# A projection by pairs in the Winograd form: other places for loads, operand sums, staging buffers and attention's first transfers

## The reference

```
h = rmsnorm(x)
q, k, v, z_att, b, c, u, z_conv, g_att, g_conv = split(h @ W_in)
A = per head: softmax(rot(q) k') v, chunk-causal, two score maps, the second subtracted times lambda
att = rmsnorm(A) * silu(z_att);       yA = att @ W_att_out
cv  = b * conv3(c * u) * silu(z_conv); yB = cv @ W_conv_out
m = sigmoid(g_att + bias0) * yA + sigmoid(g_conv + bias1) * yB
x + rmsnorm(m @ W_out)
```

## Time and profile before

| | us |
|---|---|
| median of 3 runs | 1775.97 (1775.05 to 1779.68) |
| the profiled execution | 1778.97 |
| its span in the trace | 1777.1 |
| PE busy | 1717.4 |
| DVE busy | 1042.3 |
| ACT busy | 659.2 |
| POOL busy | 250.2 |

### The profile page before, as it was taken

How to read it: one execution, slowest core, us unless ns; L and a number is a source line. 1 busy time by engine, 2 the same in 40 slices (tenths; PEclk the granted TensorE clock), 3 DMA queues, 4 the chain that set the end, 5 groups by cost and what they waited for, 6 DMA issues and landing times.

```text
span 1777.1 us, 22838 instructions
## 1 busy us (share of the span) xinstructions
PE 1717.4 (97%) x8344; PEld 1434.3 (81%) x8344; DVE 1042.3 (59%) x2087; ACT 659.2 (37%) x1168; POOL 250.2 (14%) x178
## 2 busy tenths in 40 slices
PE   7999999998999986899999998999999999999998
PEld 6888888887788875688888887888888878888887
DVE  5538655648777775366766665676766453425242
ACT  5422333224332222144444454444445452323231
POOL 0000000069322312111101112110001040000000
PEclk9999999999999998899999999999999999999999
DMA  6547999653323244976567669657666875353532
GB/s 237 154 171 299 381 349 330 216 162 107 119 78 113 71 119 121 296 219 196 186 195 226 188 206 285 202 175 226 217 210 190 275 261 185 112 189 107 182 104 77
DMA packets 169435, 343.62 MB, mean 193 GB/s; under 512 B 16097, under 2 KB 61153, under 8 KB 163809
## 3 DMA queue, kind: packets, MB, share of 16 engines
q1 hardware_dynamic: 169314, 342.06, 60.5%
HBM read 230.84 MB, written 111.16 MB: 192 GB/s over the span
## 4 chain that ended last, share of the span: by engine, by line
PE 81%; DVE 6%; POOL 4%; DMA 4%; ACT 2%; issue 2%; SPq 1%; DVEq 0%; ACTq 0%; POOLq 0%
PE bank L1402 18%; PE bank L1225 12%; PE bank L1226 12%; PE bank L1227 12%; PE bank L1362 6%; PE bank L1334 3%; PE bank L1335 3%; PE bank L1345 3%; PE bank L1307 3%; PE bank L1310 3%; PE bank L1309 3%; DMA qk_s<-stage 1%; DMA gate_s<-gate_st 1%; DVE a_op L2000 1%; PE bank L1382 1%
## 5 line engine op out<-in xcount | busy, mean ns | idle before, releaser
L1402 PE MATMUL bank<-ht,w 128*128 128x512 f32 x912 | 239.1, 397 | 0.0
L2158 DVE CUSTOM_DVE_ANT_0 e<-bank,zeros 128x512 f32<-128x512 f32 x192 | 124.9, 688 | 131.8 <-PE bank L1335 131.3
L1402 PEld LDWEIGHTS bank<-ht,w 128*128 128x128 f32 x912 | 167.8, 190 | 32.3
L1307 PE MATMUL bank<-ht,a_op 128*128 128x512 f32 x392 | 156.5, 399 | 27.6 <-DVE bank L2031 9.8
L1700 ACT ACTIVATE e<-e,nbias 128x128 f32<-128x128 f32 (+15 forms) x128 | 153.7, 1200 | 76.7 <-DVE nbias L2167 76.6
L1225 PE MATMUL bank<-ht,w 128*128 128x512 f32 x448 | 174.4, 389 | 0.8 <-issue 0.8
L1227 PE MATMUL bank<-ht,w 128*128 128x512 f32 x448 | 174.3, 389 | 0.0
L1226 PE MATMUL bank<-ht,w 128*128 128x512 f32 x448 | 174.3, 389 | 0.0
L1209 POOL TENSOR_SCALAR mask<-kc,qc 128x128 f32<-128x128 f32 (+3 forms) x64 | 87.7, 1370 | 578.0 <-DVE mx L2158 577.5
L1309 PE MATMUL bank<-ht,a_op 128*128 128x512 f32 x392 | 155.1, 396 | 0.0
L1310 PE MATMUL bank<-ht,a_op 128*128 128x512 f32 x392 | 155.0, 395 | 0.0
(11 more groups left out here) (187 smaller groups left out, 3438.9 us busy)
## 6 DMA issues: line engine op xcount, KB each, us to landing
w<-split_s SPq DMA_DIRECT2D x124, 512.0 KB, 4.8
raw<-in_w_in SPq DMA_DIRECT2D x56, 512.0 KB, 5.7
split_s<-piece SPq DMA_DIRECT2D x24, 1024.0 KB, 5.7
q_st<-qk_s SPq DMA_DIRECT2D x128, 128.0 KB, 4.7
gate_s<-gate_st SPq DMA_DIRECT2D x64, 256.0 KB, 5.2
ring<-gate_s SPq DMA_DIRECT2D x64, 256.0 KB, 3.4
ht_s<-ht SPq DMA_DIRECT2D x6, 2048.0 KB, 9.6
qk_s<-stage SPq DMA_DIRECT2D x48, 192.0 KB, 3.5
```

Of the source, the lines that this page charges most:

```text
L1307: nc.tensor.matmul(out[:], hi, right[:, k, 0, :], start=k == 0 and not adds, stop=False, skip_group_check=adds)
L1402: mm = nc.tensor.matmul(bank[2 + u % 2][:], unit_weights(u)[:, term // 2, k, :], h_slot(bb, k)[:, term % 2, :], start=i == 0, stop=i == PE ...
L2158: nc.vector.tensor_tensor_reduce(e[:, c:c + wide], bank[(0, 1, 4)[o % 3]][:, 0:wide], mask[m % 2][:, 0:wide] if masked else zeros[:, 0:wid ...
```

## The change

Eight edits, none of which adds or removes an operation on data:

1. `S_SUMS`: POOL forms S1, S2, S3, S4 in this order (it was S1, S3, S2, S4). For pairs 0 and 1 S1 and S2 stand in front of T4, S3 and S4 behind it.
2. POOL forms T3 first, from the end of tile 19's block 1 on (it waited for tile 22's block 1); T1 keeps that wait and comes second.
3. T2 lies in `u2[0]`, `u2[1]`, `tmp[2]`, `s_3[1]`; so `take_p1(1)` waits for nothing of T4 any more, and U2 of the first pairs for 14 counts of `t_sum`.
4. DVE forms U2 in front of the first two splits of a single pair.
5. SP loads pair q + 3 between the stores of blocks 2 and the stores of blocks 3 of pair q (it loaded pair q + 2 ahead of all of them); pair 4 ahead of the stores of (0, 3) and (2, 3).
6. The staging buffer of a block is two further on.
7. Before attention SP loads only the first chunk of k, stores (25, 3) and (27, 3), loads units 0 and 1, stores (25, 2) and (27, 2), and then loads the other three chunks of k.
8. v's first chunk is loaded behind the stores of (24, 2) and (26, 2).

```diff
-S_SUMS = ("S1", "S3", "S2", "S4")
+S_SUMS = ("S1", "S2", "S3", "S4")
...
-    return AT[p - 1 if kind_of(p) == "conv" and place_of(p) == 3 else p, b] % 4
+    return (AT[p - 1 if kind_of(p) == "conv" and place_of(p) == 3 else p, b] + 2) % 4
...
-        t_2 = [p1[1]] + u2 + [tmp[2]]
+        t_2 = u2 + [tmp[2], s_3[1]]
...
-        T_SUMS, T_ORDER = (1, 3, 2, 4), (1, 2, 3, 4)
+        T_SUMS, T_ORDER = (3, 1, 2, 4), (1, 2, 3, 4)
...
-            for b, x in ((3, 1), (2, 1), (3, 0)):
+            for b, x in ((3, 1), (2, 1)):
                 for q in (0, 1):
                     store_block(2 * q + x, b)
+            for x in range(2):
+                load_half_pair(4, x)
+            for q in (0, 1):
+                store_block(2 * q, 3)
             for q in range(2, X):
-                for x in range(2):
-                    load_half_pair(q + 2, x)
...
-                for b in (2, 3):
+                for x in range(2):
+                    store_block(2 * q + x, 2)
+                if q + 3 < LINE_PAIRS:
                     for x in range(2):
-                        store_block(2 * q + x, b)
+                        load_half_pair(q + 3, x)
+                for x in range(2):
+                    store_block(2 * q + x, 3)
...
-            for c in range(0, S, BLK):
-                load_k(Plan(True), 0, c)
-            sp.wait_ge(proj_done, product_at(POS[Y, "P7"]))
+            load_k(Plan(True), 0, 0)
+            for q in (X, Y):
+                store_block(2 * q + 1, 3)
             load_unit(0)
             load_unit(1)
             for q in (X, Y):
-                store_block(2 * q + 1, 3)
-            sp.wait_ge(proj_done, product_at(POS[Y, "P4"]))
-            load_v(Plan(True), 0, 0)
-            for q in (X, Y):
                 store_block(2 * q + 1, 2)
+            for c in range(BLK, S, BLK):
+                load_k(Plan(True), 0, c)
...
             for q in (X, Y):
                 store_block(2 * q, 2)
+            load_v(Plan(True), 0, 0)
...
-            pool.wait_ge(dve_done, done_at(QK_P + 2, 1))
+            pool.wait_ge(dve_done, done_at(QK_P - 1, 1))
...
-            for x in (1, 3):
-                for k in range(4):
-                    t_sums(x, k)
-            pool.wait_ge(t_sum, 4)
+            for k in range(4):
+                t_sums(3, k)
+            pool.wait_ge(dve_done, done_at(QK_P + 2, 1))
+            for k in range(4):
+                t_sums(1, k)
+            pool.wait_ge(t_sum, 8)
...
-            for x in ("S1", "S3"):
+            for x in ("S1", "S2"):
                 for q in (0, 1):
                     s_sums(q, x)
             for k in range(4):
                 t_sums(4, k)
-            for x in ("S2", "S4"):
+
+            pool.wait_ge(t_sum, 16)
+            for x in ("S3", "S4"):
                 for q in (0, 1):
                     s_sums(q, x)
...
                 if q >= 2:
                     act.wait_ge(sum_done, SUM_POS[q - 2, "U2"] + 1)
-                elif q == 1:
-
-                    act.wait_ge(t_sum, 13)
-                    act.wait_ge(ht_lo_done, 2 * NT + 5)
...
-                    dve.wait_ge(t_sum, 15)
+                    dve.wait_ge(t_sum, 14)
...
                 i = POS[q, ONE_PAIR[0]] + A_SLOTS
-                split_a(i)
-                split_a(i + 1)
                 form_u2(q)
-                split_a(i + 2)
+                for j in range(3):
+                    split_a(i + j)
                 form_u3(q)
                 form_c22(q)
                 split_a(i + 3)
```

## The result

The changed kernel takes 1769.05 us (median of 8 runs, 1765.3 to 1771.46) against 1777.0 (8 runs, 1775.05 to 1783.6): ratio 0.9943, 95% interval 0.9927 to 0.996. It is faster: by 8 us between the medians, by 0.57% (10 us) by the ratio. A gain of 23 us was forecast, and the time lies above the range. The profiled execution took 1770.07 us, its span is 1768.2.

The account below looks back on a forecast made before the run. TensorE was busy in 97% of the span, so time could come only from its idle and half-speed stretches. 3.2 + 2 + 9.1 + 9 - 0.3 = 23 us took the median from 1775.97 to 1753, range 1747 to 1764.

Parts of the forecast that it names:

- (a): Line's start: T3 first, T2 elsewhere, S2 in front of T4 bring P6 of pair 0 to 443.3, gaining 3.2 us.
- (c): Line's end: loads one pair sooner bring P5 of pair 13 to 679.4, gaining 9.1 us (7 to 10.5).
- S2 in front of S3: POOL's sums: 1.6 us less DVE waiting for P6's factor, within (c); nothing in single pairs, within (b).
- (b): Single pairs: U2 in front of the two splits removes TensorE's waits for U2, gaining 2 us (1 to 3).
- (d): Attention's start: stores in front of its loads, staging buffers turned by two, gaining 9 us (3 to 11).
- The end stays bound by transfers: Attention's start: late first weights or (26, 2) at 742 and later; (d) gives 2, total gain 16, 1760 us; 15%.
- The slow rival: Pairs' loads in front of stores of blocks 3 delay these, ACT waits for staging; 36 us lost, 1789 us; 3%.
- Those named for the line: Signs: P6 of pair 0 at 442 to 445; P3 of pair 11 waits 2 to 4 us, P5 of pair 13 8 to 10.
- the wrong side: Signs against, at attention's start: a DMA row in TensorE's waits (first weights), a 4 us wait for the maxima still there.

Follow-up runs that it names:

- load_old: Changed kernel with the old loop of loads and stores (pair q + 2 loaded ahead of pair q's stores): 1774.88 us, ratio 0.9984 to the kernel before.
- t1_first: Changed kernel with T1 formed first again and T3 behind it, both from tile 22 on: 1773.74 us in its one run.
- s3_before_s2: Changed kernel with S3 in front of S2 again for pairs 2 to 13: 1766.72 us in its one run.
- u2_old: Changed kernel with U2 behind two splits again: 1765.96 us in its one run.
- k_in_gap: Changed kernel with k's other three chunks loaded right behind the first, in the sync queue's waiting time: 1760.54 us, ratio 0.989 to the kernel before.
- line_only: Changed kernel with attention's old queue and the old staging buffers, keeping only the line's edits: 1764.82 us, ratio 0.992 to the kernel before.
- turn_old_queue: Changed kernel with attention's old queue, keeping the line's edits and the turned staging buffers: 1759.77 us, ratio 0.9883 to the kernel before.
- no_turn: Changed kernel without the turn of the staging buffers: 1774.47 us, ratio 0.9975 to the kernel before.
- last_order: turn_old_queue with the last two pairs reordered: P5, P1, P6 of pair 12, then of pair 13, then by turns: 1756.45 us, ratio 0.988 to the kernel before.

## Why the prediction was wrong

**Steps (a) and (c) held, to the microsecond.** P6 at 442.79 against 443.3 (a gain of 2.9 us without the shift between the profiles, forecast 3.2); P3 of pair 11 with 2.7 us of wait against 3. P5 of pair 13 came as forecast, but its wait is 7.2 us against 9: the two products before it took 7.3 us (granted clock 0.77 there) and not the 5.4 of the full pace, so the same time is matmuls at the lower clock and not waiting. The load as the cause is shown by load_old, T3's place by t1_first. S2 in front of S3 at pair 13 was sized at 1.6 us. From P3 of pair 11 to P5 of pair 13 it measured 2.1 (16.56 us in s3_before_s2, 14.49 in the changed kernel), but P3 came sooner in s3_before_s2, and 1.0 us is left at P5.

**Step (b) held, and one sentence in it failed.** Forecast 2 us, measured 2.2 by pair 9, and U2's place is enough to take the waits away, as s3_before_s2 shows. What failed is that S2 in front of S3 "brings nothing": by itself it does the same (u2_old), so U2's place was not needed beside it. I had looked at what S3 would now stand beside and not at what it had stood beside. The trace of before had the row: the copy of 1.25 us. The Trainium skill, page "SBUF — State Buffer", section "SBUF: two separate sides", lets VectorE's two-port copies contend with GpSimd for the port pair too, and the loser blocks for the whole instruction. By that rule a copy started beside a sum ends with the sum, and the trace agrees (507.63 and 507.61). I weighed the rule only against the change; in u2_old, where the copy stands free, it speaks for the new order of the sums.

**Step (d) failed, and with it the sum.** Forecast +9 (3 to 11), measured -1.6 in the profile, and -5 us for edits 6 to 8 alone. The failed term is this one: the stores of (26, 2), "issued by 733.9", were to "land between 738 (4 us) and 742 (8.11 us)". They were issued by 718.27, in the same coordinates 733.1, so that was right. DVE could go on at 733.22, 15 us later, not 4 to 8 (in those coordinates 748.1, not 738 to 742). I took the landing from the shortest row and from one late store, and priced it as a latency. By the experiments it is a backlog: it goes with what the transfer engines still have to move. The reason given for the short end, "the sync queue is empty from about 704 to 712", was the very fault: in the kernel before the transfer engines were full right up to the store that DVE waited for. Their share in the kernel before (columns as above):

```profile
705.00:710.00 5.00, 5.00 (x24) 4.14 (x23) 3.37 (x7) 1.43 (x3) 0.00 (x0) 1.00 0.83 188
710.00:715.00 5.00, 5.00 (x24) 4.14 (x23) 3.37 (x6) 1.53 (x3) 0.00 (x0) 1.00 1.06 239
715.00:720.00 5.00, 5.00 (x24) 4.14 (x23) 1.64 (x3) 0.60 (x1) 0.00 (x0) 1.00 1.05 272
720.00:725.00 5.00, 5.00 (x23) 4.14 (x23) 0.00 (x0) 0.00 (x0) 0.00 (x0) 1.00 1.07 321
740.00:745.00 5.00, 2.25 (x13) 1.76 (x12) 0.00 (x0) 0.60 (x1) 0.00 (x0) 1.00 1.01 350
745.00:750.00 5.00, 3.21 (x9) 2.63 (x10) 3.12 (x16) 0.88 (x4) 2.87 (x2) 0.59 0.61 222
```

Full from 710 to 745, and the earlier trace rows had the middle of it. So transfer time left unused before that stretch comes back at its end. SP's wait for block (25, 3) in front of the six other k transfers left 6.5 us unused. k_in_gap gives them back: 1760.54 against 1769.05. Counted as in (d), its first maxima gain 6.1 us (21.5 sooner than before, of which the line gave 15.4): within the 3 to 11 of (d), though not its 9.

**The rivals.** "The end stays bound by transfers" was the right one, at 15%, but its price of 7 us was too small: the true one is 10 to 11 (9 forecast, -1.6 measured). It was thought of as late landings and not as lost transfer time. The slow rival, stores delayed by the load in front of them, never showed: no wait of ACT on a stored block between 480 and 650.

**The landmarks.** Those named for the line were met but one: P5 of pair 13 waits 7.2 us, not 8 to 10. For the start of attention the wrong side came true: a DMA row in TensorE's waits (2.2 us, though for the weights of unit 2 and not for the first), a wait for the maxima of over 4 us, and ACT still waited 9.66 us for staging at 715.76.

**What stays open.** The 4 us lost between attention's start and the end in the changed kernel's profile are not explained. From the first maxima to the end of the profile line_only loses 1.4 us of its lead, k_in_gap 3.4, turn_old_queue 4.4, no_turn 0.5, and last_order gains 1.5, so the loss goes neither with the line nor with the queue alone. I tried nothing on it. Three parts of the change were not undone by themselves: T2's new place (edit 3), v's first chunk behind the stores (edit 8), and S2 in front of T4.

## What to carry to other kernels

Before a stage that opens with many megabytes, sum the volume and look at the transfer engines' share stretch by stretch: where it is full until the wait in question, a store lands when the backlog is through, and a wait of the issuing queue in front of transfers that are ready can cost much of its length (here 8.5 us of time for 6.5 us of unused transfer engines). So put loads that are already allowed into the queue's waiting time, and let the wait on a fresh block stand behind them. When one engine's work is moved, look at what it stops standing beside, not only at its new neighbours. And undo each half of a double change by itself before naming one of them the cause: here either half was enough.

## What the runs showed of the hardware

A DVE copy of 128 x 2 elements out of SBUF took 1.25 us beside a POOL sum of 1.74 us and 0.15 without it (four of each: before and u2_old). The shortest landing of a store in the stretch of the earlier trace rows was 3.5 us; DVE waited 15 us after the issue of the last stores it needed in the changed kernel, and at 265 GB/s (715 to 730) that is, as an estimate, 4 MB moved in between. In k_in_gap the transfer engines were at 0.93 to 1.03 with 203 to 234 GB/s from 690 to 705, most of it k's loads, where the kernel before had 350 GB/s at 1.01: full engines are not the same as full bandwidth.
